# Who sums modulation groups 13 to 16, and when, in a two-block diffusion transformer on Trainium2

## The reference

```python
mod = jnp.einsum('bd,ldm->lbm', jax.nn.silu(c), w_mod) + b_mod[:, None, :]
for i in range(DEPTH_2):
    sh_m, sc_m, g_m, sh_f, sc_f, g_f = [t[:, None, :] for t in jnp.split(mod[i], 6, axis=-1)]
    h = x * (1.0 + sc_m) + sh_m
    y = even_mixer(...) if i % 2 == 0 else odd_mixer(...)
    x = layer_norm_2(ALPHA * x + (1.0 + g_m) * y, ...)
    h = x * (1.0 + sc_f) + sh_f
    y = swiglu(h, w_gate[i], w_up[i], w_down[i])
    x = layer_norm_2(ALPHA * x + (1.0 + g_f) * y, ...)
```

## Time and profile before

| what | us |
|---|---|
| median of 3 runs | 1770.81 |
| span of the profiled execution, first to last instruction | 1766.3 |
| what lies around the span, against the median | 4.5 |
| TensorE busy (share of the span) | 1662.9 (94%) |
| TensorE weight loads busy | 1362.5 (77%) |
| VectorE busy | 1009.8 (57%) |
| ScalarE busy | 658.4 (37%) |
| GpSimd busy | 320.9 (18%) |

### The profile page before, as it was taken

One profiled execution on the slowest core, in us unless ns is written; L12 is line 12 of the kernel. 1 busy time (PEld: TensorE's weight loads), 2 busy tenths in 40 slices (PEclk: granted clock), 3 DMA queues, 4 the chain that ended last, 5 costly groups with the idle time before them and its releaser, 6 DMA issues.

```text
span 1766.3 us, 22795 instructions
## 1 busy us (share of the span) xinstructions
PE 1662.9 (94%) x8957; PEld 1362.5 (77%) x8957; DVE 1009.8 (57%) x1435; ACT 658.4 (37%) x887; POOL 320.9 (18%) x250
## 2 busy tenths in 40 slices
PE   4999999999999998999999999899979899999999
PEld 3897787888777875788887886677758588888877
DVE  3568798777878758533333346757576733333243
ACT  4322465432354523433222123434463533333121
POOL 0000000000000004688884011224302000000011
PEclk8999999999999999999999999999999999999999
DMA  7645200352210333456564332222002123332321
GB/s 272 214 144 191 96 1 1 115 176 85 95 55 19 96 120 103 155 183 188 181 194 131 116 103 76 77 68 65 32 25 85 61 93 96 99 102 96 114 84 48
DMA packets 145605, 187.93 MB, mean 106 GB/s; under 512 B 7053, under 2 KB 104565, under 8 KB 145524
## 3 DMA queue, kind: packets, MB, share of 16 engines
q1 hardware_dynamic: 145524, 186.82, 32.9%
HBM read 184.70 MB, written 2.10 MB: 106 GB/s over the span
## 4 chain that ended last, share of the span: by engine, by line
PE 62%; DVE 13%; POOL 9%; issue 6%; DMA 5%; ACT 4%; SPq 1%; POOLq 0%; DVEq 0%; ACTq 0%
PE ps L839 7%; PE ps L840 7%; PE ps L841 7%; POOL mraw L626 4%; POOL msum L633 4%; DMA mraw<-in_w_mod_dram 3%; PE ps L1340 2%; PE ps L1348 2%; PE ps L1341 2%; PE ps L1347 2%; PE ps L1344 2%; PE ps L1349 2%; PE ps L1403 2%; PE ps L1405 2%; PE ps L1404 2%
## 5 line engine op out<-in xcount | busy, mean ns | idle before, releaser
L1535 ACT ACTIVATE whi<-wraw 128x2048 fp32r<-128x2048 f32 x71 | 135.8, 1913 | 312.7 <-PE ps L841 216.4
L2050 DVE TENSOR_TENSOR wlo<-wraw,whi 128x2048 fp32r<-128x2048 f32 x64 | 148.2, 2315 | 157.5 <-ACT whi L1535 157.3
L2806 DVE TENSOR_TENSOR wlo<-wraw,whi 128x2048 fp32r<-128x2048 f32 x22 | 51.5, 2340 | 204.2 <-ACT whi L1899 204.2
L1340 PE MATMUL ps<-uH,whi 128*128 128x512 f32 x352 | 140.4, 399 | 10.7 <-ACT uH L1867 8.3
L839 PE MATMUL ps<-hH,whi 128*128 128x512 f32 x352 | 141.3, 402 | 0.0
L840 PE MATMUL ps<-hL,whi 128*128 128x512 f32 x352 | 140.2, 398 | 0.0
L841 PE MATMUL ps<-hH,wlo 128*128 128x512 f32 x352 | 140.0, 398 | 0.0
L1341 PE MATMUL ps<-uH,wlo 128*128 128x512 f32 x352 | 138.7, 394 | 0.0
L1347 PE MATMUL ps<-uH,whi 128*128 128x512 f32 x352 | 136.9, 389 | 0.0
L1349 PE MATMUL ps<-uH,wlo 128*128 128x512 f32 x352 | 136.9, 389 | 0.0
L1348 PE MATMUL ps<-uL,whi 128*128 128x512 f32 x352 | 136.9, 389 | 0.0
(11 more groups left out here) (500 smaller groups left out, 3830.4 us busy)
## 6 DMA issues: line engine op xcount, KB each, us to landing
mraw<-in_w_mod_dram SPq DMA_DIRECT2D x104, 512.0 KB, 3.8
wraw<-in_w_gate_dram SPq DMA_DIRECT2D x22, 1024.0 KB, 5.3
wraw<-in_w_up_dram SPq DMA_DIRECT2D x22, 1024.0 KB, 5.4
wraw<-in_w_down_dram SPq DMA_DIRECT2D x16, 1024.0 KB, 5.1
wraw<-in_w_in_dram SPq DMA_DIRECT2D x11, 1024.0 KB, 5.5
mfirst<-in_w_mod_dram SPq DMA_DIRECT2D x16, 512.0 KB, 7.3
wraw<-in_w_in_even_dram SPq DMA_DIRECT2D x8, 1024.0 KB, 5.4
wraw<-in_w_in_odd_dram SPq DMA_DIRECT2D x16, 512.0 KB, 4.6
```

What stands on the lines that cost most here:

```text
L1340: mm(o[m], w_[0][m][:, k], uH[:, k], start=(k == 0), stop=False)
L2050: V.tensor_tensor(wlo[:, n % 2, :], wraw[:, n % 2, :], whi[:, n % 2, :].bitcast(F32), ALU.subtract).then_inc(lo_done, 1)
```

## The change

Groups 13 to 16 go to POOL, at its place between the constants and the norm. Group 13 stands ahead of the zeroing of the slots, groups 14, 15 and 16 behind it. They are turned at heads 0, 2 and 4 and at item 6 of the sparse heads, no longer at head 4, items 11 and 23 and in the output product. DVE's steps for them are gone. PE's waits ahead of some transposes follow the banks that the turned groups now use.

```diff
-SB_TURN = {4: 13}
-DSA_TURN = {11: 14, 23: 15}
+SB_TURN = {0: 13, 2: 14, 4: 15}
+DSA_TURN = {6: 16}
-OUT_TURN = {0: 16}
-G_DVE = (*range(10, 18), 29)
+G_DVE = (10, 11, 12, 17, 29)
         def added(g):
-            return ps[:, 3, 256:260] if 14 <= g <= 15 else modp[:, 0:4]
+            return ps[:, 3, 256:260] if g == 16 else modp[:, 0:4]
@@ gpsimd @@
+            def early_group(g_):
+                pool.wait_ge(modT, g_)
+                for kp in range(4):
+                    pool.wait_ge(m_landed[kp % 2], 16 * (2 * (g_ - 4) + kp // 2 + 1))
+                    sum_tick(kp, kp % 2, msum_at(g_))
+
+            early_group(13)
             for i in range(8):
                 ...
                 pool.wait_ge(chunk_done, NC1 + 9 + sl)
                 g.memset(w[half, 4 * sl + 1 + e].bitcast(F32), 0.0).then_inc(zero_rd, 1)
+            for g_ in (14, 15, 16):
+                early_group(g_)
@@ tensor, sb_job @@
+                if j in (4, 6):
+                    pe.wait_ge(mod_rd, 12 + j // 2)
@@ tensor, dsa_job @@
-                    pe.wait_ge(mod_rd, 14)
-                if j >= 10:
-                    pe.wait_ge(mod_rd, 14 if j < 12 else 15)
+                    pe.wait_ge(mod_rd, 16 if j < 11 else 17)
@@ tensor, out_product @@
-                    turn = OUT_TURN.get(j) if l == 0 else None
@@ vector, stick-breaking heads @@
-                    if h < 4 and kt % 2 == 0:
-                        sum_step(13, 2 * h + kt // 2)
@@ vector, sparse heads @@
-                if i < 8:
-                    sum_step(14, i)
-                if 13 <= i < 21:
-                    sum_step(15, i - 13)
-                if i >= 25:
-                    sum_step(16, i - 25)
-            sum_step(16, 7)
@@ vector, out_steps @@
-                    if l == 0 and j in OUT_TURN:
-                        group_columns(OUT_TURN[j])
+                    if l == 0 and j == 0:
                         sum_group(17)
```

More of the change, by code:

```diff
@@ L1313, in out_product @@
                     n = n0 + j
-                    turn = OUT_TURN.get(j) if l == 0 else None
-                    product(n, use_of(n), KT, 8 * l if not j else None, uH, uL, wT[1], wT[2], turn, ready=ao_lo,
+                    product(n, use_of(n), KT, 8 * l if not j else None, uH, uL, wT[1], wT[2], ready=ao_lo,
                             near=L if j == 2 else None, ends=L if j == 3 else None)
```

## The result

The changed kernel takes 1788.07 us, the median of 5 runs (1784.49 to 1792.02), against 1770.71 us before (5 runs, 1768.73 to 1772.38). The ratio is 1.0099, with a 95% interval of 1.0084 to 1.0115: 17.4 us slower. The profiled execution took 1784.7 us; its span is 1783.0 us, against 1766.3 before. In the sets of runs further down, four single executions took 2.8 to 8.6 ms; the ratios leave them out, and they move a median by 0.1 us at most.

The account below looks back on a forecast made before the run. TensorE (PE), busy 1662.9 of 1766.3 us, was taken as the bound. Terms 13.2 - 1.4 + 3 - 0.9 = +13.9 us on the median 1770.8 gave 1784.7 us, range 1778 to 1793.

Parts of the forecast that it names:

- The forecast's case: Zeros late before the first scores, and DVE's select losing some races to POOL in the heads: 1784.7 us, chance 0.65.
- Step 1: Before the first stick-breaking scores: group 13's sum on POOL delays slot 0's zeros; PE waits 13.2 us more (11.5 to 15).
- The clock behind the long wait: After PE's wait for the zeros: half clock (0.50) lasts no longer than before; nothing taken, 0 to 2 us for the range.
- Step 2: Turns moved among stick-breaking heads, sparse heads and output product: 0.85 us each on PE, sum nought.
- Steps 3 and 4: Stick-breaking heads: DVE without sums saves PE 1.4 us; POOL's sums stopping DVE's select cost 3 us (0 to 7).
- The turns of 14 and 15: Heads 2 and 4: PE waits at most 1 us for POOL's sums, counted inside the 3 us for select.
- Step 5: Sparse heads gain nothing from removed sums; PE's wait for DVE's last output before the mixer's product shrinks, -0.9 us.
- Top-k stopped: Heads: MATCH_REPLACE8 also waits for POOL, about 11 us beyond the late zeros, 1795 us; chance 0.18 including late turns.
- Faster: First scores: zeros ready by 476.5, so DVE's relief decides; 1765.5 us with half of PE's idle time, chance 0.02.
- Partly absorbed: Zeros late, but later PE finds DVE ahead, select loses no race, half clock met less: 7.2 us, 1778, chance 0.12.

Follow-up runs that it names:

- the four with the new order: Profiles: changed kernel twice, with slot 0's zeros before group 13's sum, with half that sum before them; 68.5, 72.3, 68.0, 71.0 us from first scores to last turn.
- Three moves of order: Changed kernel with slot 0 zeroed before group 13's sum, group 15's sum after the second select, its turn at head 5: 1770.37 us, ratio 0.9999.

## Why the prediction held, point by point

The time was forecast at 1784.7 us with a range of 1778 to 1793, and measured at 1788.07. The forecast's case, the late zeros with a select that loses some, is the one that came true. Step 1 carried it; in the smaller terms some errors cancelled, as said below.

- **Step 1, the late zeros: right, and shown from both sides.** 13.2 us were forecast and 13.0 is the growth of the wait (17.24 - 4.23). The sum ended at 486.1, forecast 487.3; the landing was the sooner one. Taking it away gives back 11.3 us, adding it alone to the kernel before costs 14.5 (11.9 to 20.0) for a wait that is 15.1 us longer.
- **The clock behind the long wait: right to take nothing.** PE ran at 0.50 for 3 us behind the first scores, not longer than before.
- **Step 2, the turns: right.** 0.87 us each (532.02 to 532.89), two more in the heads, one fewer in the sparse heads and none in the product, where the table shows -0.9.
- **Steps 3 and 4, DVE relieved and DVE stopped: right in sign and nearly in size, the parts less so.** +1.6 us net was forecast, +2.2 measured at job 7. Four large instructions of the select waited, not five; the one at 534.96 met POOL at the end of an instruction. The select grew from 3.9 to 8.2 us (534.11 to 542.35), +4.3 where I had 6. The relief was smaller as well. I took DVE to run ahead by what the removed steps had cost, but it stood idle instead for 1.49, 4.56 and 1.26 us between 510 and 528, for PE and ACT, and began the select 45.6 us behind PE's first scores instead of 46.5, 0.9 us sooner with five steps gone. So PE's wait ahead of job 7 grew from 1.24 to 3.46 instead of vanishing. That the net came near is in part luck: the cost and the relief were both taken too large.
- **The turns of 14 and 15: better than feared.** I allowed 1 us of waiting; POOL had ended group 14 at 530.7 and group 15 at 551.5, 1.3 and 5.5 us before PE came, and PE waited at none of the three turns in the heads.
- **Step 5, sparse heads and tail: right.** The sums there were hidden: 6.15 against 6.16 us a head. The tail gave 0.8 to 1.2 us (the wait was 1.76 and 1.49 in the two profiles before, 0.73 in both after), forecast 0.9. Between the first scores and the mixer's product none of PE's waits over 0.6 us names a DMA.
- **What the sum lacked** is 3.4 us by the medians and 2.8 by the first profiles. The table of eight profiles has it in the heads: +6.1 us from the first scores to the last turn, where the terms make 3.3 (1.6, and two turns of 0.87). Of the 2.8 us between, 0.6 are the longer wait ahead of job 7 and 1.2 the half clock behind it; I had counted the half clock only behind the new wait, and the sum put it at nothing. About 1 is left: in the 10 us behind the scores of head 2 the granted clock was 0.83 in both profiles of the kernel before and 0.83, 0.54, 1.00 and 0.66 in the four with the new order, and whether that belongs to the change is open. The runs of the changed kernel differ by up to 7.5 us among themselves. The sum also lacked PE's wait for `Mk`, which the first profile of before didn't show.

The rivals: the top-k didn't wait, its MATCH_REPLACE8 kept 0.54 and 0.68 us beside POOL. The Trainium skill (SBUF — State Buffer, Who interferes with whom) has it that an instruction with at most one SBUF input, outside the 2-port modes, doesn't contend; if MATCH_REPLACE8 is such a one (`m` has a loading instruction of its own, MATCH_VALUE_LOAD, of 0.09 us), the trace agrees. "Top-k stopped" is thereby out. "Faster" had its deciding point at 476.5, and POOL's 17 us for a group ruled it out. "Partly absorbed" was wrong: the kernel before with POOL kept busy lost 14.5 us (11.9 to 20.0) for 15.1 of waiting.

## What to carry to other kernels

Before work is handed to an idle engine, list what that engine does in the stretch and who waits for it: here four memsets of 2.3 us in all, with 8.9 us to spare, were put behind 19 us of new work, and PE paid the difference. Relief of a busy engine is worth at most what the bounding engine waited for it, here 1.2 us at one place and 1.8 at another; it can turn into idle time ahead of the next thing that the engine needs, and the helper's own accesses can take it back. Three moves of order brought the changed kernel back to the old time, as far as the medians tell, so such a change should be measured with its order varied.

## What was not expected

- A wait of PE can cost about twice its length, as two profiles have it. The 3.65 us for group 15 was followed by 7 us at a granted clock of 0.51; with the wait gone both went, 5.4 us by the medians and 5.1 by the traces (166.8 against 161.7 us from the projection's end to the mixer's product). But the wait of 17 us, with PE idle before it for longer, was followed by only 3 us at 0.50, and the one of 4.2 us before by 5. What decides is not settled here.
- Two executions of the same changed kernel ran alike up to the scores of head 2 (508.35 and 508.50 us) and were 3.5 us apart at the suffix of head 2 (523.13 and 526.64), after equal work, at clocks of 1.00 and 0.70 in most of it. A single profile is a poor basis for a term of that size, and so is a difference of two profiles: the half clock in the first sparse heads looked like the change's doing until the kernel before showed it too, and a wait of 3.02 us was missing from the first profile of the kernel before.
- In the second select POOL and DVE alternated strictly: four DVE instructions in a row took 1.0 to 1.5 us longer than alone, never two in one gap of POOL. The last of the four reads one SBUF tensor only (`work`, written out as bf16), and waited as the others did.
